# The exchange of half heads in a rotary embedding: by transfers within the scratchpad, or by matmuls

## The reference, cut to what matters

```python
def _rope(t, pos):                     # t (B, S, H, 64)
    half = t.shape[-1] // 2
    freqs = ROPE_THETA ** (-jnp.arange(half) / half)
    ang = pos[:, None] * freqs[None, :]
    cos, sin = jnp.cos(ang)[None, :, None, :], jnp.sin(ang)[None, :, None, :]
    t1, t2 = t[..., :half], t[..., half:]
    return jnp.concatenate([t1 * cos - t2 * sin, t2 * cos + t1 * sin], axis=-1)

oc = _dsa(_rope(cq), _rope(ck), cv, _rope(cqi), _rope(cki), cwi)
# _dsa: iscore[t, s] = sum_h w[t, h] * relu(qi[t, h] . ki[s]); the 256 best admissible
# keys s of each token t are kept; softmax attention of q over those keys
```

## Time and profile before

| | |
|---|---|
| median of 3 runs | 3019.27 us (3017.55 to 3020.47) |
| the profiled execution's own time | 3018.58 us |
| its span in the profile | 3016.8 us |
| TensorE clock granted, mean | 0.993 |
| PE busy | 2883.6 us |
| VectorE busy | 1560.9 us |
| ScalarE busy | 970.7 us |
| GpSimd busy | 813.8 us |

### The profile page before, as it was taken

The page is one execution under the profiler, slowest core; times in us unless marked ns, Lnnn a source line. Parts: engine busy times, 40 slices in busy tenths (PEclk is TensorE's granted clock), DMA queues, the critical chain, the costliest instruction groups (busy, mean ns, idle before and its releaser), DMA issues. The chain is left out here.

```text
span 3016.8 us, 46711 instructions
## 1 busy us (share of the span) xinstructions
PE 2883.6 (96%) x18888; PEld 1541.7 (51%) x18888; DVE 1560.9 (52%) x3173; ACT 970.7 (32%) x1836; POOL 813.8 (27%) x572
## 2 busy tenths in 40 slices
PE   7998999999999999999999989999999999999998
PEld 3446454575544465444445464545755444654443
DVE  2587867533358812155226878674333598030643
ACT  2255663211133324300113556632111333253001
POOL 2026412312133232232020353133021332322320
PEclk9999999999999999999999999999999999999999
DMA  5001101101121221263040011011010212212631
GB/s 213 18 28 37 42 24 44 51 16 40 33 76 39 77 85 65 91 212 112 0 140 18 29 42 42 20 51 43 16 43 34 81 33 93 80 46 94 228 100 56
DMA packets 132493, 195.80 MB, mean 65 GB/s; under 512 B 8088, under 2 KB 88120, under 8 KB 132024
## 3 DMA queue, kind: packets, MB, share of 16 engines
q1 hardware_dynamic: 113688, 158.74, 16.3%
q10 hardware_dynamic: 18592, 34.09, 3.0%
HBM read 146.14 MB, written 48.78 MB: 65 GB/s over the span
## 5 line engine op out<-in xcount | busy, mean ns | idle before, releaser
L509 PE MATMUL ps<-hT,wr 128*128 128x512 f32 x1600 | 748.8, 603 | 0.5 <-issue 0.5
L509 PEld LDWEIGHTS ps<-hT,wr 128*128 128x128 f32 x1600 | 289.8, 191 | 306.2 <-issue 298.0
L509 PE MATMUL ps<-sums,wr 128*128 128x512 f32 x800 | 383.0, 607 | 4.5 <-ACT gts L579 4.5
L660 POOL TENSOR_TENSOR gts<-gts,wr 128x512 f32<-128x512 f32 x96 | 134.9, 1406 | 633.5 <-ACT wr L560 484.2
L509 PEld LDWEIGHTS ps<-sums,wr 128*128 128x128 f32 x800 | 145.4, 193 | 155.0 <-issue 145.1
L738 PE MATMUL ps<-xo,arena 128*128 128x512 f32 x512 | 220.1, 592 | 0.0
L635 POOL TENSOR_TENSOR wr<-wr 128x512 f32<-128x512 f32 (+1 forms) x56 | 87.2, 1558 | 450.6 <-PE ps L509 320.7
L1137 DVE CUSTOM_DVE_ANT_0 arena<-ps,arena 128x640 f32<-128x640 f32 (+7 forms) x128 | 90.4, 706 | 213.8 <-PE ps L1038 196.0
L509 PE MATMUL ps<-wr 128*128 128x512 f32 x400 | 191.6, 602 | 6.5 <-ACT wr L560 6.5
L1507 DVE TENSOR_SCALAR_CACHE_REDUCE arena<-arena,sm 128x384 f32<-128x384 uint16 (+7 forms) x256 | 192.8, 810 | 2.2
L560 ACT ACTIVATE wr<-ps 128x512 f32<-128x512 f32 x150 | 89.1, 594 | 303.5 <-PE ps L509 289.3
(11 more groups left out here) (316 smaller groups left out, 4714.5 us busy)
## 6 DMA issues: line engine op xcount, KB each, us to landing
wr<-in_w_in SPq DMA_DIRECT2D x68, 1024.0 KB, 5.4
gate_tanh<-gts ACTq DMA_DIRECT2D x128, 256.0 KB, 2.1
arena<-gate_tanh SPq DMA_DIRECT2D x128, 256.0 KB, 3.0
x_cur<-arena SPq DMA_DIRECT2D x2, 4096.0 KB, 24.3
arena<-in_w_branch SPq DMA_DIRECT2D x8, 1024.0 KB, 9.8
wr<-in_w_out SPq DMA_DIRECT2D x8, 1024.0 KB, 6.9
arena<-x_cur SPq DMA_DIRECT2D x4, 2048.0 KB, 8.8
arena<-in_x SPq DMA_DIRECT2D x4, 1024.0 KB, 8.3
```

Of the source, the lines that this page charges most:

```text
L509: ins = pe.matmul(ap, lhsT=right(u, w_side)[:, kt, :], rhs=left(h_side, kt), start=fresh and kt == 0, stop=kt == half_k - 1, skip_group_ch ...
L660: pool.tensor_tensor(dst, dst, stage_of(u), ALU.add).then_inc(sg("pool_added"), 1)
```

## The change

- `rot`, `pe_rope` and the 18 calls a layer go. `pe_proj_t` has nothing behind its pieces but the transposition of the head weights, once. The sine table has its sign flipped in the lower half of each head.
- The partners are fetched by transfers within the scratchpad, issued by SP: one of 32 partitions x 1024 for each half head, so four for a block of 128 partitions and two for ki (`sp_turn`). `sp_index` does it for the five blocks of the indexer, each into a buffer of its own or one that `roped` shows to be free, `sp_qk` for q and for k as wholes of 128 x 2048, into one shared buffer (k's waits until q is rotated). Their places in SP's order come from `sp_turns`.
- DVE rotates each indexer block in three operations on 1024 tokens (five blocks) in place of three on 512 (ten halves). ACT's eight copies go. POOL rotates q and k in the same 24 operations, at places counted in fills behind the end of the block's projection.
- On PE, 9 fills stand between the last projection piece and the wait for `roped`, in place of 12 between rotary calls; beside the search 181 fills run in a row, in place of 178. The sum of both is 190 as before, so each fill behind the search has its old place.
- ACT's schedule `beside` loses the term for rotary calls, and its stop at step 16 is 100 fills instead of 92.

```diff
-TOPK_FILL = 70
-QK_FILL = 8
-ROPE_FILL = 3
-QK_ROPE_FILL = 4
-ROPE_BITS = (3, 4, 5, 6, 10, 11, 12, 13)
+TOPK_FILL = 181
+ROPE_FILL = 9
...
+    cs[(r // half) % 2 == 0, 1] *= -1
...
-                turned = [H(16.25, 0.5), H(16.75, 0.5)]
+                turned = [H(16.25), H(17.25), H(18.25), H(17.25), H(18.25)]
+                qk_turned = U(17.25)
...
+                def sp_turn(sp, dst, x, rows, sem):
+                    for r in range(0, rows, HD // 2):
+                        other = r + HD // 2 if r % HD == 0 else r - HD // 2
+                        sp.dma_start(dst[r:r + HD // 2], x[other:other + HD // 2]).then_inc(sem, 16)
+
+                def sp_index(n):
+                    name, buf, m, col = roped[n]
+                    def load(sp, l):
+                        for half in range(2):
+                            jobs.stored(sp, raw_key(name, m, half))
+                        if n >= 3:
+                            sp.wait_ge(sg("roped"), n - 1)
+                        sp_turn(sp, turned[n], buf[:, col, :], rows_of(name), sg(f"turned{n}"))
+                    return load
+
+                def sp_qk(j):
+                    def load(sp, l):
+                        unit_done(sp, ("C", 4 + j))
+                        if j == 0:
+                            sp.wait_ge(sg("index_sums"), 2 * len(index_units))
+                        else:
+                            sp.wait_ge(sg("qk_roped"), 4)
+                        sp_turn(sp, qk_turned, (q, k)[j], P, sg(f"qk_turned{j}"))
+                    return load
...
-                    for m in range(2):
-                        for half in range(2):
-                            pe_rope(pe, "qi1", m, half)
-                            pe_fill(pe, ROPE_FILL)
-                    pe.wait_ge(sg("roped"), 2 * len(index_roped))
+                    pe_fill(pe, ROPE_FILL)
+                    jobs.mark("index roped")
+                    pe.wait_ge(sg("roped"), len(roped))
...
-                        passed = 13 + (26 * k) // 5 + 2 * half - ropes - 2 * (k >= 10) + 12 * (k >= 16)
+                        passed = 13 + (26 * k) // 5 + 2 * half - 2 * (k >= 10) + 12 * (k >= 16)
...
+                        pool_fills(pool, ("beside search", unit_ended[j] + 6 + 5 * (n % 4)))
                         if n % 4 == 0:
-                            jobs.stored(pool, last_key(unit_of["C", 4 + n // 4]))
+                            pool.wait_ge(sg(f"qk_turned{j}"), 16 * 4)
...
+                        dve.wait_ge(sg(f"turned{n}"), 16 * (rows // (HD // 2)))
+                        dve.tensor_tensor(t, t, cs[0:rows, 1, :], ALU.mult)
+                        link(dve, dve.tensor_tensor(x, x, cs[0:rows, 0, :], ALU.mult))
+                        dve.tensor_tensor(x, x, t, ALU.add).then_inc(sg("roped"), 1)
```

More of the change, by code:

```diff
@@ L102, in constants @@
     put("diag2", (t % HD) == np.arange(HD)[None, :])
[L103 to L110, removed]
     half = HD // 2
@@ L449, in pe_proj_t @@
                         jobs.filled(ins, key)
-                        behind[2 * m + half](pe)
+                        if behind is not None and (m, half) == (0, 0):
+                            behind(pe)
                 block_done[n] = key
@@ L1297, in rows_of @@
                     return HD if name == "ki" else P
[L1299 to L1305, removed]
-                    r = rows_of(name)
-                    jobs.filled(pe.matmul(ap[0:r, :], lhsT=C("rot")[0:r, 0:r], rhs=buf[0:r, col, 512 * half:512 * half + 512],
-                                          start=True, stop=True), key)
+                def sp_turn(sp, dst, x, rows, sem):
+                    for r in range(0, rows, HD // 2):
+                        other = r + HD // 2 if r % HD == 0 else r - HD // 2
+                        sp.dma_start(dst[r:r + HD // 2], x[other:other + HD // 2]).then_inc(sem, 16)
@@ L1310, in mixer_c, with sp_turns @@
+                def sp_turns():
+                    return [(raw_key(roped[n][0], roped[n][2], 1), sp_index(n)) for n in range(len(roped))] \
+                        + [(last_key(unit_of["C", 4 + j]), sp_qk(j)) for j in range(2)]
                 searched = [0]
-                def beside_search(pe, n, unit=None):
-                    while n or not (unit is None or unit in unit_of and last_key(unit_of[unit]) in jobs.fills_by):
-                        if unit is None or unit in unit_of and last_key(unit_of[unit]) in jobs.fills_by:
-                            n -= 1
+                unit_ended = {}
@@ L1317, in beside_search @@
+                def beside_search(pe, n):
+                    for _ in range(n):
                         pe_fill(pe, 1)
                         jobs.mark(("beside search", searched[0]))
+                        for j in range(2):
+                            if j not in unit_ended and ("C", 4 + j) in unit_of and last_key(unit_of["C", 4 + j]) in jobs.fills_by:
+                                unit_ended[j] = searched[0]
                         searched[0] += 1
@@ L1466, in dve @@
                     dve.wait_ge(sg("cs_loaded"), 16)
[L1467 to L1470 removed]
+                    dve_rope(dve)
+                    dve.wait_ge(sg("roped"), len(roped))
                     for n, (i, hp, c, w) in enumerate(index_units):
```

73 lines of the change are left out of this document (19 added, 54 removed).

## The result

The kernel before took 3019.86 us (median of 4 runs, 3017.55 to 3020.47), the changed one 2999.93 us (4 runs, 2998.57 to 3003.82): a ratio of 0.9938 [0.9920, 0.9955], 20 us less where 24.4 were forecast. Run again with five runs it took 2998.0 us, 0.9932 [0.9920, 0.9945]. The profile is of the slowest of the four, 3003.82 us.

What follows compares the result with a forecast made beforehand. The prediction took TensorE (PE), busy 96% of the span, to bound the kernel. Terms of 12.2 + 0 + 0 us a layer gave 24.4 in the launch and 2995 us; likeliest range 2985 to 3003, 8 in 10 from 2983 to 3007.

Steps and rivals of the forecast that it cites:

- Projections and the last block's chain: From projections to first index score: 5.6 us off in the projections, 6.6 up to the score, 12.2 a layer.
- The term for landings: Last index block ahead of the scores: four 128 KB transfers land in 4.2 us, plus 0.1 for the wake-up.
- PE's visible wait: Ahead of the first index score: PE waits 1.5 us for DVE's rotation of the last block.
- the prediction's other estimate: Last index block's landing by the skill page: 2.4 us behind a fixed 2, 4.4 in place of 4.2.
- Rival 2: Last block's transfers come one behind the other: 11.6 for 4.3, 9.8 us gained in all, 3009; chance 0.10.
- q's transfer: In the search: wanted 1 us later, landed 4 later, so POOL loses 3 and begins where it began before.
- The search at 0: Five PE slots fewer change nothing in the search; bounds 7.9 + 0.9 better to 3 worse.
- 173 us as before within 1.5: Sign in the profile: the search, from last index score to attention's first DVE operation, keeps its length.
- Rival 1: PE paces the search, so five freed slots come off: 4.3 us a layer more, 33 in all, 2986; chance 0.22.
- The gap ahead of attention C: At attention C's start: PE idles 2.5 to 3 us where it idled 0.8 at most.
- Rival 3: POOL hangs on q's and k's transfers in the search: landings of 18.9 us, 24 a layer lost, 3042; chance 0.06.
- The rest only shifts: Behind attention C's start: every fill stands where it stood, so nothing differs there, 0 us.

Runs made afterwards that it cites:

- run 1: The changed kernel measured again, unedited: 0.9932 of the kernel before, 2998.0 us.
- run 9: The changed kernel with the last index block's four transfers made twice, the second group after the first has landed: 3012.68 us, 0.9978 of the kernel before.
- run 4: The changed kernel with three fills put back ahead of the wait for `roped` (12 and 178 instead of 9 and 181): 2997.41 us, 0.9928 of the kernel before.
- run 2: The changed kernel with only the index blocks by transfers, q and k keeping their rotary matmuls: 2996.67 us, 0.9928 of the kernel before.
- run 3: The kernel before with only q and k by transfers, the index blocks keeping their rotary matmuls: 3023.67 us, 1.0018 of the kernel before.
- run 7: The changed kernel with q's and k's transfers in two groups of four 128 KB pieces, POOL waiting for each: 2996.98 us, 0.9924 of the kernel before.
- run 8: The changed kernel with each group of q's and k's transfers made twice, the second after the first has landed: 3020.11 us, 1.0001 of the kernel before.
- run 6: The changed kernel with ScalarE asked to empty three slots fewer at each search step: 2995.90 us, 0.9921 of the kernel before.
- run 5: The changed kernel with four more fills ahead of attention C (185 instead of 181), ScalarE's schedule unchanged: 2992.82 us, 0.9910 of the kernel before.
- run 12: The changed kernel with q's and k's transfers in two groups and four more fills ahead of attention C: 2989.43 us, 0.9899 of the kernel before.

## Why the prediction was right, step by step

**Projections and the last block's chain: right.** 12.2 a layer forecast; 11.95 in layer 1 and 11.29 in layer 2 in run 1's trace. The two terms err both ways. From the first projection matmul to the first rotary call or fill behind the last piece it is 60.7 us before and 55.7 in run 1: 5.0 off for 5.6. ki's two calls were priced at 1.52 each from the distance of weight loads; PE's own timeline before has 1.00 from one's start to the next matmul:

```profile
52.62 1.07 PE L1307 MATMUL ps<-arena,con 64*64 64x512 f32 x2
53.62 7.13 PE L447 MATMUL ps<-hT,wr 128*128 128x512 f32 x16
```

From there to the first score 17.45 us became 10.57: 6.9 off for 6.6. The term for landings, 4.3 with the wake-up, measured 4.18; PE's visible wait was 0.77 instead of 1.5. By the Trainium skill, "SBUF — State Buffer", section "Door 1: The DMA port swizzle", with the fixed 2 us of its section "The DMA setup-cost knee", the prediction's other estimate was 4.4, and the trace agrees within 0.2. Rival 2 is out, and run 9 prices it higher than it was put: 1.6 us of time for one of landing, as the clock falls behind a wait of 4.9.

**q's transfer: mis-sized, and wanted earlier.** The prediction had it "wanted 1 us later and landed 4 later: POOL loses 3". POOL wanted it 1.1 us ahead of the issue, and it landed 6.8 behind it: a wait of 7.96. Of the 5 us missed, 2.8 are the size and 2.1 the order. q is two blocks of 128x1024, 1 MB in four pieces of 256 KB, where an index block is half that; the prediction carried the index blocks' 4 us over. Worked as it had worked that block, the last issue (3 x 0.75 us) and one piece's landing (3.9), it would have had 6.2. By the same page of the Trainium skill, sections "Door 1: The DMA port swizzle" and "The DMA setup-cost knee", 1 MB at 218 GB/s would be 4.8 us behind a fixed 2, an estimate of 6.8; the trace agrees to 0.1, though no run here shows the rate by itself.

**The search at 0: wrong in its reasons.** It came out 2.3 and 2.5 us a layer longer, just inside the bound of "3 worse" and outside the "173 us as before within 1.5" that was to be seen in the profile (175.6). The forecast balanced waits of PE in slots and took the fills' new place as free ("three steps earlier in their order and cost the same"). It wasn't: the fill that releases POOL's sum came later among the scores, and DVE ended 3.7 us later against PE (runs 1 and 4). From that later end on the search is 1.3 us shorter than before, so what it lost against the last score is a later begin, less what it caught up. In exchange run 1's scores gave 1.0 and 2.1 us, forecast 0: ahead of the last scores PE no longer waits the 1.4 us for ScalarE, which waited for a DVE held by the clash.

**Why eight freed slots bought nothing.** Rival 1 is out: q and k only was slower, and 189 slots were no slower than 181 (runs 2 and 3). The gap ahead of attention C was forecast at 2.5 to 3, "where it idled 0.8 at most", and is 3.9, with 5.1 where the clash is put back. The reason given was that ScalarE's schedule in slots paces the end. Runs 7 and 8 show that POOL's rotation of k does, one for one, in the changed kernel: k begins 1.9 and 2.1 us later against the last score than in the kernel before, and the search is 2.3 and 2.5 longer. Whether the schedule takes over once POOL is out of the way is open. Run 6 moved both, and with the fills first the search gave only 4.2 us for 6.8 of POOL.

**Rival 3: the mechanism works, its size is small.** The prediction named over 5 us of POOL's waiting as its sign, and it is 8. It took the price of one for one right and the landings of 18.9 wrong: they are 6.8. Run 8 brings it to the point where it decides: with POOL 6.8 us later at q and 10.3 at k the gain is zero, near the "some 12 us lost in all" of the prediction (11.4 and 10.1 a layer).

**Behind attention C's start: not the same.** "The rest only shifts" left out the clock. In the changed kernel's first profiled execution the rest is 4.2 us longer than in the kernel before, in its repeat 0.5. Summed over windows of 50 us, the granted clock gives 30.1 us at half the clock in that stretch of the first execution and 23.4 in the repeat: 6.7 more, worth 3.4 us, nearly all of the 3.6 between the two. It doesn't account for the kernel before, whose stretch has 15.9; what makes up for it there is open.

**Sum.** In run 1: 23.2 off for the 24.4 forecast, 3.1 more in the scores, 4.9 back in the search, 0.5 in the rest. The forecast of 2995 is 3 to 5 us short of 2998.0 and 2999.9, and part of that closeness is luck: the longer search was partly hidden by gains in the scores that nobody had forecast, and the 0.6 too much in the projections in part by a last chain shorter than forecast.

## What to carry to other kernels

Before counting freed slots, find which engine paces the stretch: here DVE's last sum started the search and POOL's rotation of k paced it, so PE's freed slots turned into one idle, and only work moved into that idle made time of it (four fills did; six, together with other edits, lost it again). When work changes places in an order, look at what waits for a place in it, POOL's long sum here, and where its operation then meets an engine it holds up. Size every transfer by its own bytes: the same four-way exchange took 4.2 us for 512 KB and 6.8 for 1 MB.

## What the runs showed of the hardware

- A wait of PE can cost more than its length. Behind idles of 3.9 to 5.1 us (runs 1, 3, 4 and 9) the clock fell to 1.2 GHz, behind the 1.1 ahead of attention C (runs 5 and 12) it did not. The length alone doesn't decide, not even in one kernel. At 231.05 the changed kernel idled 2.00 us and then took 5.38 for 16 matmuls; its repeat idled 1.99 and took 3.69. The same in its scores, first execution, then repeat:

```profile
127.66 1.53 PE L1369 MATMUL ps<-arena 64*128 64x512 f32 x8 [1.93 <-ACT arena L1394]
129.11 3.46 PE L471 MATMUL ps<-wr,hT 128*128 128x256 f32 x8
...
127.12 1.35 PE L1369 MATMUL ps<-arena 64*128 64x512 f32 x8 [1.95 <-ACT arena L1394]
128.40 1.99 PE L471 MATMUL ps<-wr,hT 128*128 128x256 f32 x8
```

- Transfers within the scratchpad, 32 partitions each: a piece of 128 KB lands 2.9 us after its issue in the median of the changed kernel's 36 (2.3 for the 68 of the split one), a piece of 256 KB 3.9, and four of these 6.8 us after the first issue.
- A POOL sum of 4.5 us on 128x2048 elements held one DVE operation of 0.75 us for 5.0.
